# A hybrid decoder layer on one core: another order for its opening and its first pair of heads

## What is computed

```
h = rmsnorm(x, g_mix)                      # x: 512 x 1024
q_sb, k_sb, v_sb, q_r, k_r, v_r, g_r, gate_sb, gate_ret = split_cols(h @ w_in)
q_sb, k_sb = head_rmsnorm(q_sb), head_rmsnorm(k_sb)     # 8 heads of 64
y_sb = stick_breaking_attention(q_sb, k_sb, v_sb)
q_r, k_r = rotary(q_r), rotary(k_r) * 64 ** -0.5
y_r = head_rmsnorm(retention_chunkwise(q_r, k_r, v_r)) * silu(g_r)
x += (sigmoid(gate_sb) * (y_sb @ w_a) + sigmoid(gate_ret) * (y_r @ w_b)) @ w_out
x += (gelu(causal_dwconv3(h2 @ w_gate)) * (h2 @ w_val)) @ w_down   # h2 = rmsnorm(x, g_ffn)
x += sigmoid(rmsnorm(x, g_ple) @ w_pg) * (p @ w_pp)
```

## Time and profile before

| | us |
|---|---|
| median of 3 executions | 911.59 |
| the 3 executions | 911.5, 911.59, 914.9 |
| the profiled execution | 913.93 |
| its span, from first to last instruction | 912.1 |

### The profile page before, as it was taken

The page is one execution under the profiler, slowest core; times in us unless marked ns, Lnnn a source line. Parts: engine busy times, 40 slices in busy tenths (PEclk is TensorE's granted clock), DMA queues, the critical chain, the costliest instruction groups (busy, mean ns, idle before and its releaser), DMA issues.

```text
span 912.1 us, 11455 instructions
## 1 busy us (share of the span) xinstructions
PE 892.4 (98%) x4070; PEld 724.4 (79%) x4070; DVE 517.4 (57%) x660; ACT 398.9 (44%) x519; POOL 4.0 (0%) x11
## 2 busy tenths in 40 slices
PE   6998999999999999999999999999999999999998
PEld 5776787787787888888887888888888888888786
DVE  6787577577677453333555666566655643333354
ACT  6636657557566442233244433333333332223431
POOL 1000000000000000000000000000000000000000
PEclk9999999999999999999999999999999999999999
DMA  7214214214213153322322332222222232322141
GB/s 275 80 36 139 81 36 138 80 35 138 80 35 127 58 196 104 104 82 91 115 94 96 115 111 92 92 92 92 100 107 92 86 104 87 103 86 93 58 143 70
DMA packets 28553, 89.93 MB, mean 99 GB/s; under 512 B 3920, under 2 KB 4960, under 8 KB 28400
## 3 DMA queue, kind: packets, MB, share of 16 engines
q1 hardware_dynamic: 27232, 85.87, 27.4%
q10 hardware_dynamic: 1072, 3.67, 1.2%
q0 software_dynamic: 224, 0.06, 0.1%
HBM read 84.34 MB, written 2.10 MB: 95 GB/s over the span
## 4 chain that ended last, share of the span: by engine, by line
PE 92%; DVE 4%; ACT 2%; issue 1%; DMA 1%; SPq 0%; ACTq 0%; DVEq 0%
PE dense L346 29%; PE dense L348 28%; PE dense L347 28%; PE z L402 2%; DVE fs L1068 1%; DVE w_lo L1068 1%; PE aty L431 1%; DVE fs L1071 1%; PE aty L446 1%; PE aty L391 1%; ACT fs L629 1%; ACT w_hi L644 1%; DMA fs<-in_xT 1%; PE aty L348 1%; PE aty L347 1%
## 5 line engine op out<-in xcount | busy, mean ns | idle before, releaser
L346 PE MATMUL dense<-hi,w_hi 128*128 128x512 f32 x1184 | 471.3, 398 | 9.3 <-DVE lo L1071 8.9
L348 PE MATMUL dense<-hi,w_lo 128*128 128x512 f32 x1184 | 462.7, 391 | 0.0
L347 PE MATMUL dense<-lo,w_hi 128*128 128x512 f32 x1184 | 462.6, 391 | 0.0
L1068 DVE TENSOR_TENSOR w_lo<-w_f,w_hi 128x1024 fp32r<-128x1024 f32 (+2 forms) x160 | 184.3, 1152 | 229.4 <-ACT w_hi L644 228.9
L346 PEld LDWEIGHTS dense<-hi,w_hi 128*128 128x128 f32 x1184 | 223.3, 189 | 60.4 <-issue 13.3
L348 PEld LDWEIGHTS dense<-hi,w_lo 128*128 128x128 f32 x1184 | 223.1, 188 | 47.4
L347 PEld LDWEIGHTS dense<-lo,w_hi 128*128 128x128 f32 x1184 | 223.5, 189 | 44.4 <-issue 1.2
L644 ACT CAST w_hi<-w_f 128x1024 fp32r<-128x1024 f32 (+2 forms) x160 | 158.3, 990 | 181.3 <-PE dense L348 179.0
L629 ACT ACTIVATE fs<-fs 128x512 f32<-128x512 f32 (+2 forms) x79 | 55.3, 707 | 80.7 <-DVE fs L1068 41.5
L1068 DVE TENSOR_TENSOR fs<-fs 128x512 f32<-128x512 f32 (+2 forms) x119 | 87.7, 742 | 3.9 <-ACT fs L676 0.5
L1068 DVE TENSOR_TENSOR lo<-fs,hi 128x512 fp32r<-128x512 f32 (+3 forms) x73 | 54.5, 755 | 40.9 <-ACT hi L1003 20.1
(11 more groups left out here) (87 smaller groups left out, 379.8 us busy)
## 6 DMA issues: line engine op xcount, KB each, us to landing
w_f<-in_w_in SPq DMA_DIRECT2D x52, 512.0 KB, 3.3
w_f<-in_w_up SPq DMA_DIRECT2D x44, 512.0 KB, 3.1
w_f<-in_w_down SPq DMA_DIRECT2D x16, 512.0 KB, 3.5
w_f<-in_w_b SPq DMA_DIRECT2D x8, 512.0 KB, 3.2
w_f<-in_w_out SPq DMA_DIRECT2D x8, 512.0 KB, 3.2
w_f<-in_w_pg SPq DMA_DIRECT2D x8, 512.0 KB, 3.2
w_f<-in_w_down SPq DMA_DIRECT2D x8, 384.0 KB, 3.0
fs<-in_xT SPq DMA_DIRECT2D x4, 512.0 KB, 7.0
```

The source lines that it names most:

```text
L346: mm(out, w1, x1, start=start, stop=False, skip_group_check=skip)
L347: mm(out, w1, x0, start=False, stop=False, skip_group_check=skip)
L348: return mm(out, w0, x1, start=False, stop=stop, skip_group_check=skip)
L1068: return nc.vector.tensor_tensor(out, a, b, op).then_inc(done, 1)
```

## The change

The opening, the first pair and nothing else are written in another order; the loop over pairs 1 to 3 and all after it are as before (its table of `places` is only written elsewhere). Part by part:

- **Zero products.** DVE clears the tile `hi[:, T_SQ]` after `eps`, and PE multiplies it with itself ten times (`warm_up`) into `aty` bank 2 ahead of chunk 0.
- **Loads.** SP loads the first half of chunk 0's weights (256 KB), x tiles 0 and 1 alone (256 KB each), the second half, and then x in pairs as before. That is seven DMAs ahead of chunk 1's where there were five. ACT and DVE split the weights in two halves, the second ahead of x tile 2.
- **The norm of x.** `stat_x` moves from tile 6 of chunk 1 to tile 2 of chunk 2. Two of DVE's `raw_sum` come after the `low` of chunk 2, and `low` of chunk 3 comes before the constants.
- **Rows for q and k.** `a_raw` gives q and k of the first pair the rows `A_G` and `A_G + 1`, so that they don't share `A_RAW` with later slots. DVE empties both and does their head norm ahead of any `normed`; ACT follows. `sb_scores` stays at tile 7 of slot 3.
- **Two more banks.** Slots 3 and 4 go to `aty` banks 1 and 2, and of the first pair only slots 5 and 8 wait for a bank. `sb_turn(0, 0)` waits for slot 3 to be emptied and `sb_values(0, 0, 3)` for slot 4.
- **Places and lists.** Attention's group 1 and 2 scores, `sb_turn(0, 0)` and the first `sb_values` hang 1 to 2 tiles earlier or later. In `first_back` the steps `high_h(2)` to `high_h(7)` and their DVE partners stand between the attention steps in another order.

The diff, cut to its core:

```diff
-            def load_x(i):
-                sp.dma_start(fs[:, A_X + 2 * i:A_X + 2 * i + 2, :], xT[:, 2 * i:2 * i + 2, :]).then_inc(s_x[i], 16)
-
-            load(0, 0, w_in[0], 8, first=True)
-            for i in range(4):
-                load_x(i)
+            sp.dma_start(w_f[0][:, 0:4, :], w_in[0][:, 0:4, :]).then_inc(s_w0, 16)
+            for i in range(2):
+                sp.dma_start(fs[:, A_X + i, :], xT[:, i, :]).then_inc(s_x[i], 16)
+            sp.dma_start(w_f[0][:, 4:8, :], w_in[0][:, 4:8, :]).then_inc(s_wdma[0], 16)
+            for i in range(1, 4):
+                sp.dma_start(fs[:, A_X + 2 * i:A_X + 2 * i + 2, :], xT[:, 2 * i:2 * i + 2, :]).then_inc(s_x[i + 1], 16)
             load(1, 1, w_in[1], 8, first=True)
             sp.dma_start(cst[:, :, :], consts).then_inc(s_cst, 16)
             load(2, 2, w_in[2], 8, first=True)
...
-            def chunk(c, r, b, kt, tile0, hooks=None, k_first=0, last=True, before=None):
-
-                pe.wait_ge(s_wlo, c + 1)
+            def chunk(c, r, b, kt, tile0, hooks=None, k_first=0, last=True, before=None, out=None):
+
...
                     pe.wait_ge(s_raw_done, RAWS * j + 3)
-                    if not isinstance(j, int):
+                    if isinstance(j, int):
+                        pe.wait_ge(s_evac, 4)
+                    else:
                         pe.wait_ge(s_misc, 3 * j + 2)
...
                 if hd == 0 and kb == NT - 1:
                     pe.wait_ge(s_raw_done, RAWS * j + 3)
-                    if not isinstance(j, int):
+                    if isinstance(j, int):
+                        pe.wait_ge(s_evac, 5)
+                    else:
                         pe.wait_ge(s_yraw, j)
                 if hd == 1 and kb == NT - 1:
...
+            def warm_up():
+
+                pe.wait_ge(s_warm, 1)
+                for _ in range(10):
+                    mm(aty[:, 2, :], hi[:, T_SQ, 0:P], hi[:, T_SQ, :], start=True, stop=True)
...
+                    places = {(3, 1): at(stat_qk, 0, 1, (s_misc, 1)), (3, 7): at(sb_scores, j, 0),
+                              (4, 2): at(turn_v, 0, 2, (s_misc, 2)), (5, 0): at(sb_scores, j, 1),
+                              (5, 2): at(sb_turn, j, 0), (5, 7): at(sb_values, j, 0, 3), (6, 1): at(sb_scores, j, 2),
+                              (6, 3): at(sb_turn, j, 1), (7, 0): at(sb_values, j, 0, 2), (7, 3): at(sb_turn, j, 2),
+                              (7, 6): at(sb_values, j, 0, 1), (7, 7): at(sb_values, j, 0, 0)}
+                    later = 1
...
+                places[8, later] = at(sb_values, j, 1, 3)
+                places[8, later + 1] = at(sb_values, j, 1, 2)
+                places[8, later + 2] = at(sb_values, j, 1, 1)
+                places[8, later + 3] = at(sb_values, j, 1, 0)
+                places[8, 6] = at(turn_v, j, 7, (s_atlo, 3 * j + 3))
                 for s in range(3, SLOTS):
-                    free_bank(j, s)
+                    if prev is not None or s in (5, 8):
+                        free_bank(j, s)
...
+                    out = aty[:, s - 2, :] if prev is None and s in (3, 4) else None
+                    chunk(SLOTS * j + s, s % RING, s % 3, KD, T_X0 if raw else T_H, hooks, before=before, out=out)
...
+            warm_up()
             chunk(0, 0, 0, KD, T_X0, before={k: (s_xlo, k + 1) for k in range(KD)})
-            chunk(1, 1, 1, KD, T_X0, {6: stat_x})
-            chunk(2, 2, 2, KD, T_X0, {7: lambda: stat_qk(0, 0, (s_xrs, 1))})
+            chunk(1, 1, 1, KD, T_X0)
+            chunk(2, 2, 2, KD, T_X0, {2: stat_x, 7: lambda: stat_qk(0, 0, (s_xrs, 1))})
...
+            act.wait_ge(s_w0, 16)
+            nc.scalar.copy(w_hi[0][:, 0:4, :], w_f[0][:, 0:4, :]).then_inc(s_w0hi, 1)
             act.wait_ge(s_gmix, 16)
             for k in range(KD):
-                if k == 0:
-                    high(0, 0, first=True)
-                if k % 2 == 0:
-                    act.wait_ge(s_x[k // 2], 16)
+                if k == 2:
+                    act.wait_ge(s_wdma[0], 16)
+                    nc.scalar.copy(w_hi[0][:, 4:8, :], w_f[0][:, 4:8, :]).then_inc(s_whi, 1)
+                if k < 2 or k % 2 == 0:
+                    act.wait_ge(s_x[(0, 1, 2, 2, 3, 3, 4, 4)[k]], 16)
...
                 high(0, 2, first=True)
+                ahead(0, 1)
                 act.wait_ge(s_xst, 1)
                 run(fs[:, A_RS, :], misc, ACT.Ln, s_xln, scale=1.0 / D, bias=eps[:, :])
                 act.wait_ge(s_xln, 1)
                 run(fs[:, A_RS, :], fs[:, A_RS, :], ACT.Exp, s_xrs, scale=-0.5)
-                high_h(0)
-                ahead(0, 1)
-                high_h(1)
+                ahead(0, 2)
                 norm_qk(0, 0, 1)
-                ahead(0, 2)
                 high_qk(0, 0)
                 norm_qk(0, 1, 2)
+                high_qk(0, 1)
                 sigmoid_tables()
-                high_qk(0, 1)
-                high_h(2)
-                high_h(4)
+                high_h(0)
+                high_h(1)
+                ahead(0, 3)
             def high_h(k):
                 act.wait_ge(s_hf, H_ORDER.index(k) + 1)
...
                 sb_factors(0, 0)
-                ahead(0, 3)
                 high_v(0, 0)
-                high_h(3)
+                high_h(2)
                 ahead(0, 4)
-                high_h(5)
+                high_h(4)
                 sb_high(0, 0)
                 sb_factors(0, 1)
+                high_h(3)
                 ahead(0, 5)
                 sb_high(0, 1)
+                high_h(5)
                 sb_factors(0, 2)
+                ahead(0, 6)
                 high_h(6)
-                ahead(0, 6)
                 sb_high(0, 2)
                 high_rot(0, 0)
                 y_out(0, 0)
...
             nc.vector.memset(eps[:, :], EPS).then_inc(s_eps, 1)
+            nc.vector.memset(hi[:, T_SQ, :].bitcast(F32), 0.0).then_inc(s_warm, 1)
...
-                    dve.wait_ge(s_raw_done, RAW_OF[s] - 1)
-                dst = A_RAW + RAW_OF[s] % 2 if s in RAW_OF else A_G + s - 5
-                tt(fs[:, dst, :], bank[s % 3][:, :], fs[:, A_RS, :], ALU.mult, s_evac)
+                    dve.wait_ge(s_h, 2)
+                    if s == 4:
+                        dve.wait_ge(s_raw_done, 3)
+                    elif s == 7:
+                        dve.wait_ge(s_raw_done, 4)
+                    dst = A_RAW + RAW_OF[s] % 2
+                else:
+                    dve.wait_ge(s_raw_done, 2)
+                    dst = A_G + s - 5
+                src = aty[:, s - 2, :] if s in (3, 4) else bank[s % 3][:, :]
+                tt(fs[:, dst, :], src, fs[:, A_RS, :], ALU.mult, s_evac)
             def square(j, t):
...
             def start():
                 dve.wait_ge(s_xrs, 1)
+                dve.wait_ge(s_cr, 7)
+                evac_x(0)
+                square(0, 0)
+                evac_x(1)
+                square(0, 1)
+                ahead(0, 2)
+                norm(0, 0)
+                low_qk(0, 0)
+                norm(0, 1)
+                low_qk(0, 1)
                 normed(0)
                 normed(1)
                 low_h(0)
-                evac_x(0)
-                square(0, 0)
-                ahead(0, 1)
                 low_h(1)
-                evac_x(1)
-                square(0, 1)
-                normed(2)
-                norm(0, 0)
-                ahead(0, 2)
-                low_qk(0, 0)
-                norm(0, 1)
-                low_qk(0, 1)
-                low_h(2)
-                normed(4)
                 evac_x(2)
+                ahead(0, 3)
                 dve.wait_ge(s_rope, 16)
             def turned(j, t):
...
             def first_back():
-                low_h(4)
-                ahead(0, 3)
-                normed(3)
                 sb_weights(0, 0)
                 evac_x(3)
                 low_v(0, 0)
-                low_h(3)
-                normed(5)
+                normed(2)
                 ahead(0, 4)
                 evac_x(4)
-                low_h(5)
+                normed(4)
+                low_h(2)
+                low_h(4)
                 sb_low(0, 0)
                 sb_weights(0, 1)
+                normed(3)
                 ahead(0, 5)
                 evac_x(5)
+                low_h(3)
                 sb_low(0, 1)
+                normed(5)
                 sb_weights(0, 2)
+                ahead(0, 6)
+                evac_x(6)
+                low_h(5)
                 normed(6)
-                ahead(0, 6)
                 sb_low(0, 2)
-                low_h(6)
-                normed(7)
-                evac_x(6)
                 turned(0, 0)
                 low_rot(0, 0)
+                low_h(6)
                 ahead(0, 7)
+                normed(7)
+                evac_x(7)
                 low_h(7)
-                evac_x(7)
                 turned(0, 1)
                 low_rot(0, 1)
                 ahead(0, 8)
```

53 lines of the change are left out of this document (29 added, 24 removed).

## The result

The changed kernel takes 918.18 us (median of 6 executions, 917.6 to 919.83). The kernel before, timed beside it, takes 914.59 (median of 6, 911.5 to 915.04). The ratio is 1.0051, with a 95% interval of 1.0033 to 1.007: slower by 3.6 us. The executions of before lie in two heaps, 911.3 to 912.2 and 913.0 to 915.3, so its median moves with the share of each. In later comparisons it was 913.05 (13 executions) and 912.13 (24). In these 37 the mean granted clock of the whole execution is 1.0 for every one of the lower heap and 0.996 to 0.998 for every one of the upper, the profiled one (0.998) among them. The profiled executions are 918.6 against 913.93.

What follows compares the result with a forecast made beforehand. The order of steps in ACT's and DVE's in-order lists was taken to bound the first pair. DVE's terms, -0.3 + 3.1 + 3.3 - 1.9 + 0.9, gave +5.1 us; 911.6 + 5.0 and some 0.3 more gave 917.0, range 913.5 to 920.0.

Steps and rivals of the forecast that it cites:

- block 1: DVE, end of `sb_low(0, 0)` to start of `sb_low(0, 1)`: 9.2 us instead of 6.1, +3.1.
- block 2: DVE, from there to the start of `sb_low(0, 2)`: 9.9 us instead of 6.6, +3.3.
- block 3: DVE, from there to the start of `turned(0, 0)`: only `sb_low`, 0.6 us instead of 2.5, -1.9.
- block 4: DVE, from there to the start of `turned(0, 1)`: 8.1 us instead of 7.2, +0.9.
- block 5: DVE, `turned(0, 1)` to `low_rot(0, 1)`: 3.55 us, unchanged.
- The lead is down to 0.3 us.: First pair: of PE's 1.6 us lead at group 0's scores, 0.3 remains when `sb_low(0, 0)` ends, about 52.5 instead of 52.8.
- Nothing is given back: Loop over pairs 1 to 3 and the rest: the same as before, so none of the loss is recovered there.
- I take no clock loss: PE's waits in the first pair, 2 to 3 us each: parted by products, so no clock loss was charged.
- The clock rises late: Rival, opening: zero products don't count or clock rises mid chunk 0; `A_RS` 1 us later, 918.0 to 918.5; chance 0.17.
- The blocks cost half: Rival, first pair: the first two DVE stretches cost 3.2 us instead of 6.4, time 913.8; chance 0.2.
- PE sets the pace: Rival, first pair: DVE's chain ends before PE gets there, the opening's gain of 1.6 to 2.6 us stays, 909.6; chance 0.1.
- The warm-up is the whole story: Rival, opening: full clock from the first product and no other loss, gaining 1.9 plus 2.6 us, time 907.1; chance 0.03.

Runs made afterwards that it cites:

- e3: The changed kernel with only the first_back lists of ACT and DVE in another order, no high_h ahead of steps ready sooner: 909.96 us, ratio 0.9971.
- e1: The changed kernel with the loads of the kernel before (chunk 0's weights whole, x in four pieces of 512 KB): 918.02 us, ratio 1.0061.
- e2: The changed kernel without the ten zero products and the memset they wait for: 917.89 us, ratio 1.0056.
- e6: The kernel before with only its first_back lists mended in the same way as e3: 909.08 us, ratio 0.9962.
- e9: e6 with twenty zero products ahead of chunk 0: 908.63 us, ratio 0.995 to the kernel before.
- e7: e3 with the loads of the kernel before and twenty zero products instead of ten: 908.9 us, ratio 0.9955 to the kernel before.
- e5: The changed kernel with one step of ACT's list moved, high_h(5) behind sb_factors(0, 2) instead of ahead of it: 916.34 us, ratio 1.0036.
- e11: e3 without the two extra PSUM banks, every slot waiting for its bank: 909.82 us, ratio 0.9965 to the kernel before.

## Why the prediction was right, and where it was not

The forecast was 917.0, and 918.18 was measured, in its range; the cause it named, the order of the two lists, is the one that the runs showed. By its steps:

**The blocks on DVE** held, each within 0.2 us.

| | forecast | measured in after | 
|---|---|---|
| block 1 | 9.2 | 62.97 - 53.97 = 9.0 |
| block 2 | 9.9 | 72.81 - 62.97 = 9.84 |
| block 3 | 0.6 | 73.41 - 72.81 = 0.60 |
| block 4 | 8.1 | 81.46 - 73.41 = 8.05 |
| block 5 | 3.55 | 85.16 - 81.46 = 3.70 |
| waits for w_hi in the list | 1.7 twice | 1.63 and 1.63 |
| wait ahead of group 2's scans | 1.9 | 1.80 |
| wait for `sb_high(0, 2)` | 1.3 | 1.17 |

They are short sums of row durations, and what could be wrong in them was only who waits for whom. That is in the two lists and in no row of the trace of before.

**The opening** is the step that failed: "The lead is down to 0.3 us." By it `sb_low(0, 0)` should have ended at 52.5; it ended at 52.68 + 1.29 = 53.97, 1.15 later than before instead of 0.3 sooner. The first real product came as forecast (6.3, measured 6.62). The term that was too small is `A_RS`: 25.0 to 25.7 forecast, 27.2 measured. It rests on "chunk 1 can start at 15 us at the earliest", for which x had to land as before. Chunk 1 started at 17.34 and `A_RS` was ready 9.9 us behind that (in e3 15.97 and 25.86, the same distance). The sign "the scores of group 0 start before 35.5" failed with it: they started at 36.45. x did not land as before. ACT, on its x tiles and the second half of the weights:

```profile
7.15 0.72 ACT L654 ACTIVATE hi<-fs,gain 128x512 fp32r<-128x512 f32 x1 [1.45 <-DMA fs<-in_xT]
8.51 0.62 ACT L683 CAST w_hi<-w_f 128x512 fp32r<-128x512 f32 x1 [0.64 <-DMA w_f<-in_w_in]
9.74 0.72 ACT L654 ACTIVATE hi<-fs,gain 128x512 fp32r<-128x512 f32 x1 [0.61 <-DMA fs<-in_xT]
...
26.60 0.63 ACT L654 ACTIVATE fs<-fs 128x512 f32<-128x512 f32 x1
```

Tile 2 starts there at 9.74. In the kernel before, the same row is:

```profile
8.02 1.33 ACT L629 ACTIVATE hi<-fs,gain 128x512 fp32r<-128x512 f32 x2 [0.20 <-DMA fs<-in_xT]
```

And the clock was low until 15.3. The profiled e3 has the same opening and parts the two: there tile 2 starts at 8.67 on ACT and its first product at 10.23 instead of 11.30, 1.07 us sooner, and the clock is back at 13.7; `A_RS` is 1.37 sooner. So between these two executions 1.1 us is the landing of x and 0.3 is what came behind it. From `A_RS` on the interval to the scores was forecast as 9.2 to 9.9 (34.9 less 25.0 to 25.7) and was 36.45 - 27.2 = 9.2. So the lead of 1.6 us at the scores was 0.1, from one wrong input. e1 mended that input and the median hardly moved, so the miss of 1.2 us in the time can't be put down to the landing alone.

**"Nothing is given back" in the loop** held: 830.8 against 830.6 us.

**"I take no clock loss"** failed as a statement and cost the sum nothing. From 68 to 76 us the clock was granted at 0.74 and 0.84, behind PE's wait of 1.99 at `sb_turn(0, 2)`, but PE still came to `r_scores` 1.13 us early and waited for `low_rot(0, 1)`. The list set the time there, not PE. In e1 such a stretch fell at 56, where PE's transposes are what DVE needs next, and there it cost 0.6 us.

**The waits of PE**: 3 us forecast at the first `sb_values`, 2.48 measured; the two others were forecast at 2 to 2.5 each and came to 1.45 together, since PE had already lost 1.99 at `sb_turn(0, 2)` for DVE's product. Neither that wait nor the one of 1.18 at `sb_scores(0, 2)` was in the forecast.

**The rivals.** "The clock rises late" did happen (15.3), its condition that chunk 1 starts at 16 to 17 was met and passed (17.34), and the time lies in its 918.0 to 918.5. So the result is the forecast's lists with this rival's late `A_RS` on top; which part of the 1.2 us is the clock was not shown, as x landed late in the same execution. e2, without zeros, has the same late clock and the same time, so the zeros neither helped nor harmed. "The blocks cost half" is ruled out by the table. "PE sets the pace" needed DVE's lists 6.5 us shorter; e3 took 8.1 off them (`low_rot(0, 1)` ends at 76.39 instead of 85.85, less the 1.4 of `A_RS`), and its 909.96 is near the 909.6 of that rival. But even there PE waits 0.68 us for `low_rot(0, 1)` at `r_scores`, so DVE still comes last, by little; only in e6 and e9 does PE come to `r_scores` without a wait. "The warm-up is the whole story" is ruled out by e2, and by e7 and e9, in which the zeros do all that they can. The Trainium skill advises to warm up with products first (TensorE: Matmul & The Clock Gate, Why this matters for your kernels). Here that gave full rate through all of chunk 0 only with the twenty zeros of e7 and e9, which ran up to the first real product, and then it was worth 0.5 us (e9 against e6), within the ranges.

**The choice between profiled execution and median** mattered as much as a block. I added 3.3 to one and 5.0 to the other. 918.6 - 913.93 = 4.7 was measured for the profiled pair and 918.18 - 914.59 = 3.6 for the medians, because before's executions come in two heaps and the share of the upper one changes from comparison to comparison. The chances suffered from the same: 918.18 is above the line of 916.2, to which I gave 0.58, but that line was counted from a median of 911.6. Against the 914.59 beside it the difference is 3.6 us, under the 4.6 that I took as the least to be told, and that case had 0.38. Which of the two came out was settled by before's heaps, not by the change.

What stays open: how much of the 0.9 us between e3 and e6 is the loads, the later `stat_x` or chance; and whether e1's executions that weren't profiled had its lead of 1.3 us at all, since e3 had an `A_RS` of 25.9 with the small pieces too.

## What to carry to other kernels

Where two engines with in-order lists hand work to each other, look for a step that idles for an input while what stands behind it has its input ready. Such a pair of rows names the line to move, and moving it was worth about the idle time of the one who waits where one line was moved: 1.8 us for a wait of 1.80. Thirteen moved steps, which took away four waits of 6.2 us together and more besides, were worth 8.2. An earlier first product, ten zero products and two more banks brought nothing that shows beside it. And a step that isn't urgent (here the norm of a slot needed 20 us later) belongs behind the urgent ones on **both** engines: its producer and its consumer both hold up the line.

## What was not expected of the hardware

**The clock falls again behind a warm-up.** Ten zero products (1.50 to 5.7) brought it up in the change, and while the real ones came one tile at a time with idle times of about 1 us between them it went back to half until 15.3. None of these idle times is over 1.13 us. It isn't the same each time: with the same ten zeros the first tile still ran at 0.43 in e5 and e11 and the second at 0.23. With twenty, ending 0.4 us ahead of the real ones, it stayed at full: in e9 no two products of a tile are more than 0.34 us apart from 8.63 on. Read this from the pace and not from the PEclk number, which in the first microseconds doesn't tell the two apart. In the kernel before it says 1.00 from 9 to 10 us too, where the products follow at 0.43:

```profile
9.00:10.00 1.00, 1.00 (x3) 0.78 (x3) 1.00 (x2) 1.00 (x3) 0.00 (x0) 1.00 1.03 393
```

**With the small pieces the DMA engines were less busy.** Busy times by stretch of the change, the last two numbers being DMA share and GB/s:

```profile
4.00:5.00 1.00, 1.00 (x3) 0.79 (x3) 0.69 (x1) 0.28 (x2) 1.00 (x3) 1.00 0.65 206
5.00:6.00 1.00, 0.69 (x3) 0.19 (x1) 0.19 (x1) 0.70 (x1) 0.07 (x1) 1.00 0.53 118
6.00:7.00 1.00, 0.38 (x2) 0.34 (x3) 0.56 (x1) 0.00 (x0) 0.00 (x0) 1.00 0.67 249
```

In the kernel before the shares of these three are 1.00, 0.88 and 1.01. As a mean over the three it is 0.62 to 0.83 in the five profiled kernels with the small pieces and 0.90 to 0.97 in the five with the large ones. The first x tile comes some 2 us sooner, but ACT starts on tile 2 at 9.4 to 10.0 in four of five profiled kernels with the small pieces (8.7 in e3) and at 8.0 to 8.7 in five with the large ones. The landing also varies by itself: with the same opening `A_RS` was ready at 25.9, 26.6, 27.2 and 28.5 us in four executions (e3, e11, the change, e5). So one profile can't settle a difference between two openings of a microsecond or two.
